# One copy of the row sums instead of two, with each 128-row scatter cut into two transfers of 64 rows

## What is computed

```python
def hier_moe(x, ...):                       # first block; the second one's is alike, with TOP_K 8 of 64
    ...                                     # e: expert of each (token, choice); c: its weight
    order = jnp.argsort(e_flat)             # pairs (token, choice) sorted by expert, padded
    def expert_block(args):
        xb, e = args
        hb = jax.nn.silu(xb @ w_gate[e]) * (xb @ w_up[e])
        return hb @ w_down[e]
    y = lax.map(expert_block, (x_pad, blk_expert)).reshape(P, D).astype(jnp.float32) * c_pad[:, None]
    out = jax.ops.segment_sum(y, tok_pad, num_segments=T + 1)[:T]
```

## Time and profile before

| | |
|---|---|
| time, median of 3 runs (us) | 3725.83 (3720.07 to 3726.52) |
| the profiled execution's own time (us) | 3724.51 |
| its span, first to last instruction (us) | 3722.8 |
| TensorE busy | 3232.0 us, 87% |
| VectorE, ScalarE, GpSimd busy | 42%, 19%, 20% |
| granted TensorE clock, mean | 0.934 |
| DMA, mean of the span | 152 GB/s |
| scatter L1767 | 103 transfers, 1756 ns of GpSimd each |
| gather L1746 | 109 transfers, 1069 ns of GpSimd each |

### The profile page before, as it was taken

How to read it: one execution, slowest core, us unless ns; L and a number is a source line. 1 busy time by engine, 2 the same in 40 slices (tenths; PEclk the granted TensorE clock), 3 DMA queues, 4 the chain that set the end, 5 groups by cost and what they waited for, 6 DMA issues and landing times. The chain is left out here.

```text
span 3722.8 us, 44810 instructions
## 1 busy us (share of the span) xinstructions
PE 3232.0 (87%) x14083; PEld 1609.1 (43%) x14084; DVE 1579.9 (42%) x2344; ACT 725.6 (19%) x1144; POOL 760.5 (20%) x952
## 2 busy tenths in 40 slices
PE   5999879995988996899869996798799999999991
PEld 2444345543655444433347774355333333333330
DVE  2222224434766123434436664234344444444445
ACT  2212213333544000111122320021011111111111
POOL 0000000002000000334510000000155555555554
PEclk9999989997999998799979997898899999999995
DMA  4111031113211123799650002202488999888875
GB/s 166 36 33 39 0 126 46 46 54 77 69 47 48 67 98 135 281 384 383 232 133 23 23 11 76 96 31 83 159 289 286 312 325 342 279 279 288 278 223 165
DMA packets 177131, 564.53 MB, mean 152 GB/s; under 512 B 18597, under 2 KB 88841, under 8 KB 139913
## 3 DMA queue, kind: packets, MB, share of 16 engines
q1 hardware_dynamic: 140888, 428.46, 30.4%
q0 software_dynamic: 35856, 133.74, 14.7%
q10 hardware_dynamic: 288, 1.05, 0.1%
HBM read 460.01 MB, written 103.20 MB: 151 GB/s over the span
## 5 line engine op out<-in xcount | busy, mean ns | idle before, releaser
L1814 PE MATMUL gu_ps<-w_gu,second 128*64 x1680 | 754.0, 602 | 12.9 <-DVE h L1877 7.7
L1817 PE MATMUL gu_ps<-h,second 128*64 128x512 f32 x1680 | 754.0, 602 | 0.0
L1814 PEld LDWEIGHTS gu_ps<-w_gu,second 128*64 128x64 f32 x1680 | 224.0, 138 | 454.5 <-issue 442.6
L1840 PE MATMUL y_ps<-w_dn,hid_t 128*64 x824 | 375.6, 598 | 0.3 <-issue 0.2
L1843 PE MATMUL y_ps<-second,hid_t 128*64 128x512 f32 x824 | 375.6, 598 | 0.0
L396 PE MATMUL ps<-second,wcol 128*128 128x512 f32 x768 | 333.7, 597 | 10.1 <-DMA wcol<-in_w_in_dram 7.7
L1877 DVE COPY h<-w_gu 128x4096 f32 x109 | 249.4, 2289 | 72.2 <-SPq L1694 71.9
L1742 POOL COPY idx<-moe_slot_tok 128x1 int32 (+1 forms) x109 | 25.1, 231 | 1024.9 <-POOLq L95 984.4
L396 PEld LDWEIGHTS ps<-second,wcol 128*128 128x128 f32 x768 | 147.0, 192 | 195.8 <-issue 187.9
L1817 PEld LDWEIGHTS gu_ps<-h,second 128*64 128x64 f32 x1680 | 224.0, 138 | 0.0
L1762 POOL TENSOR_TENSOR idx_y<-moe_slot_tok,moe_side 128x1 int32<-128x1 int32 x103 | 109.7, 1065 | 521.2 <-ACT second L1863 521.2
(11 more groups left out here) (430 smaller groups left out, 5085.4 us busy)
## 6 DMA issues: line engine op xcount, KB each, us to landing
w_gu<-in_w_gate_dram SPq DMA_DIRECT2D x96, 1024.0 KB, 8.1
w_gu<-in_w_up_dram SPq DMA_DIRECT2D x96, 1024.0 KB, 10.9
w_dn<-in_w_down_dram SPq DMA_DIRECT2D x96, 1024.0 KB, 10.5
wcol<-in_w_in_dram SPq DMA_DIRECT2D x12, 1024.0 KB, 5.3
qk_by_head<-stage SPq DMA_DIRECT2D x32, 384.0 KB, 3.3
qk<-qk_by_head SPq DMA_DIRECT2D x16, 768.0 KB, 7.6
token_sums<-zero POOLq DMA_DIRECT2D x19, 512.0 KB, 13.6
token_sums<-second SPq DMA_DIRECT2D x16, 512.0 KB, 2.6
```

The costliest lines, as they stand in the source:

```text
L1814: nc.tensor.matmul(gu_ps[0:PART, slot], x_t[:, slot, c, 0:PART], w_gu[:, bass.ds(ws, 1), :, c, :].rearrange("p o g n -> p (o g) n"), start ...
L1817: last = nc.tensor.matmul(gu_ps[PART:P, slot], x_t[:, slot, c, PART:P], st_gu[:, slot, :, c, :], start=c == 0, stop=c == C - 1)
L1840: nc.tensor.matmul(y_ps[0:PART, cs], hid_t[:, slot, c, 0:PART], w_dn[:, bass.ds(ws, 1), c, cs].rearrange("p o n -> p (o n)"), start=c == 0 ...
```

## The change

There is one copy of the sums, and no two transfers that add to it are in the air together. Each block's scatter is now two transfers of 64 rows (`part(slot, 0)` for partitions 0 to 63, `part(slot, 1)` for 64 to 127). The second is issued when the first has landed (`scatter_rest`), and the first of the next block when the second of this one has landed. `G.pair` holds the row numbers of both halves on partitions 0 to 63. The order within GpSimd's queue stays scatter, share, gather, and the second half comes behind the gather. The zeroing of the second copy and the adding of it are gone. ScalarE waits for 32 instead of 16 on `y_out` for each block. The last turn gathers one block more than before.

```diff
-def zero_second(pool, sum_d, zero, zero_out):
-
-    for t in range(T + 1):
-        pool.dma_start(sum_d[S + P + t * P:S + P + (t + 1) * P, :], zero).then_inc(zero_out, 16)
...
-def add_second(pool, sum_d, rows, row_in, both_in):
-    for t in range(T):
-        pool.wait_ge(row_in[t], 16)
-        pool.dma_start(rows[:, t, :], sum_d[S + P + t * P:S + P + (t + 1) * P, :],
-                       accum_op=ALU.add).then_inc(both_in[t], 16)
...
@@ take_sums
-                pe.wait_ge(both_in[t], 16)
+                pe.wait_ge(row_in[t], 16)
...
@@ dispatch
-            st(d.tensor_scalar(side[:], G.tok[:, 0:1], float(PART), float(S + P), ALU.is_ge, ALU.mult))
...
-            st(d.tensor_copy(G.side, side[:]))
...
+            for a in range(2):
+                st(d.tensor_copy(G.pair[:, 0:NB, a], empty[a * PART:(a + 1) * PART, :]))
...
@@ experts
-            def scatter(b, slot, landed, others):
+            def scatter(b, slot, own, others):
 
                 pool.wait_ge(y_taken, b + 2)
-                if landed is not None:
-                    pool.wait_ge(y_out[slot], landed)
-                g.tensor_tensor(idx_y[:, slot:slot + 1], G.slot_tok[:, bass.ds(b, 1)], G.side, ALU.add).then_inc(idx_y_ready, 1)
+                if own is not None:
+                    pool.wait_ge(y_out[slot], own)
+                g.tensor_copy(idx_y[:, slot, :], G.pair[:, bass.ds(b, 1), :].rearrange("p o a -> p (o a)")).then_inc(idx_y_ready, 1)
                 pool.wait_ge(idx_y_ready, 2 * b + 1)
                 if others is not None:
                     pool.wait_ge(y_out[1 - slot], others)
                 g.tensor_tensor(mark_y[:, slot:slot + 1], G.tok[:, 0:1], G.tok[:, 0:1], ALU.add).then_inc(idx_y_ready, 1)
-                g.indirect_dma_start(sum_d, bass.IndirectOffsetOnAxis(ap=idx_y[:, slot:slot + 1], axis=0),
-                                     y[:, slot, :], None, compute_op=ALU.add).then_inc(y_out[slot], 16)
+                part(slot, 0)
+
+            def scatter_rest(slot, landed):
+
+                pool.wait_ge(y_out[slot], landed)
+                g.tensor_tensor(mark_b[:, slot:slot + 1], G.tok[:, 0:1], G.tok[:, 0:1], ALU.add).then_inc(mark_ready, 1)
+                part(slot, 1)
+
+            def part(slot, a):
+                g.indirect_dma_start(sum_d, bass.IndirectOffsetOnAxis(ap=idx_y[:, slot, a:a + 1], axis=0),
+                                     y[a * PART:(a + 1) * PART, slot, :], None, compute_op=ALU.add).then_inc(y_out[slot], 16)
...
                     with pool.If(i <= n + 1):
-                        pool.wait_ge(x_turned, i)
-                        pool.wait_ge(share_in, i)
-                        gather(i + 1, 1 - slot)
-                        scatter(i - 2, slot, j * 16 + 16, j * 16 + (16 + 16 * u))
+                        scatter(i - 2, slot, j * 32 + 32, j * 32 + (32 + 32 * u))
                         keep_share(i, slot, j * 16 + 48)
...
+                        pool.wait_ge(x_turned, i + 1)
+                        pool.wait_ge(share_in, i + 1)
+                        gather(i + 2, slot)
+                        scatter_rest(slot, j * 32 + 48)
...
@@ final_norm
-            add_second(pool, sum_d, G.h, row_in, both_in)
...
-                v.wait_ge(both_in[t], 16)
+                v.wait_ge(row_in[t], 16)
```

More of the change, by code:

```diff
@@ L319, in _, with lru @@
                                 gain[:, :, None].to_broadcast([P, C, P]), ALU.mult).then_inc(taken, 1)
-def zero_second(pool, sum_d, zero, zero_out):
-    for t in range(T + 1):
-        pool.dma_start(sum_d[S + P + t * P:S + P + (t + 1) * P, :], zero).then_inc(zero_out, 16)
-def lru(nc, A, G, spare, sum_d):
+def lru(nc, A, G, spare):
     ph = phase(nc)
@@ L383, in _ @@
                 pool.dma_start(rows[S:S + P, :], zero[:, 0:rows.shape[1]]).then_inc(zero_out, 16)
-            zero_second(pool, sum_d, zero[:, 0:D], zero_out)
-            pool.wait_ge(zero_out, 16 * (len(spare) + T + 1))
+            pool.wait_ge(zero_out, 16 * len(spare))
         @block.tensor
@@ L1229, in take_sums @@
         row_in = ph.sems(" ".join(f"row_in{t}" for t in range(T)))
-        both_in = ph.sems(" ".join(f"both_in{t}" for t in range(T)))
         block = ph.ctx.enter_context(nc.Block())
@@ L1236, in _ @@
                 sp.dma_start(rows[:, t, :], sum_d[t * P:(t + 1) * P, :]).then_inc(row_in[t], 16)
-        @block.gpsimd
-        def _(pool):
-            add_second(pool, sum_d, rows, row_in, both_in)
         @block.tensor
@@ L1773, in _ @@
             n = pool.value_load(G.used, min_val=0, max_val=NB)
-            keep_share(0, 0, 16)
-            for i in range(1, 4):
-                pool.wait_ge(x_turned, i)
-                pool.wait_ge(share_in, i)
-                gather(i + 1, (i + 1) % 2)
+            for i in range(4):
                 if i >= 2:
-                    scatter(i - 2, i % 2, None, 16 if i == 3 else None)
+                    scatter(i - 2, i % 2, None, 32 if i == 3 else None)
                 keep_share(i, i % 2, i // 2 * 16 + 16)
+                pool.wait_ge(x_turned, i + 1)
+                pool.wait_ge(share_in, i + 1)
+                gather(i + 2, i % 2)
+                if i >= 2:
+                    scatter_rest(i % 2, 16)
             with pool.Fori(0, (NB - 1) // 2) as j:
@@ L1912, in moe_state @@
     G.w = w[:].rearrange("p (t k) -> p t k", k=K)
-    G.side = sb(f"moe_side{E}", [P, 1], I32)[:]
+    G.pair = sb(f"moe_pair{E}", [PART, P, 2], I32)[:]
     G.m = sb(f"moe_m{E}", [P, T, E])[:]
@@ L2228, in _, with pooling @@
             take_out(H - 1, H)
-def pooling(nc, A, G, sum_d):
+def pooling(nc, A, G):
     ph = phase(nc)
@@ L2247, in pooling @@
         p_ps = ph.ps("p_ps", [P, 2, S])
-        zero = ph.sb("zero", [P, D])
-        w_in, wp_in, u_ready, u_taken, m_ready, p_ready, p_taken, dve, cleared, zero_out = ph.sems(
-            "w_in wp_in u_ready u_taken m_ready p_ready p_taken dve cleared zero_out")
+        w_in, wp_in, u_ready, u_taken, m_ready, p_ready, p_taken, dve = ph.sems(
+            "w_in wp_in u_ready u_taken m_ready p_ready p_taken dve")
         block = ph.ctx.enter_context(nc.Block())
-        @block.gpsimd
-        def _(pool):
-            nc.gpsimd.memset(zero[:], 0.0).then_inc(cleared, 1)
-            pool.wait_ge(cleared, 1)
-            zero_second(pool, sum_d, zero[:], zero_out)
-            pool.wait_ge(zero_out, 16 * (T + 1))
         @block.sync
@@ L2628, in program @@
         rms_to_cols(nc, G, vec(G, "norm_mix_g"), G.u)
-        lru(nc, A, G, (rows1_d, rows2_d, sum_d), sum_d)
+        lru(nc, A, G, (rows1_d, rows2_d, sum_d))
         mla_project(nc, A, G, qk_d, v_d)
@@ L2653, in program @@
             hgrn(nc, A, G)
-            pooling(nc, A, G, sum_d)
+            pooling(nc, A, G)
             moe_state(nc, moe, G, K2, E2)
```

25 lines of the change are left out of this document (13 added, 12 removed).

## The result

| | before | after |
|---|---|---|
| median of the runs | 3726.2 us | 3968.7 us |
| range of the runs | 3720.1 to 3726.9 | 3948.7 to 3972.7 |
| ratio, 95% interval | | 1.0644 [1.0607, 1.0681] |
| span of the profiled execution | 3722.8 | 3966.3 |

The kernel became 6.4% slower. Forecast were 3714 us and a range of 3698 to 3800. The table by stretch of the kernel after, for the two expert stages (from the first gather to the reads that follow), shows where it went. The columns are: stretch, length, busy time (instructions) of TensorE, its weight loads, VectorE, ScalarE and GpSimd, then the share of TensorE's full clock that was granted, the DMA engines' busy share, GB/s.

What follows compares the result with a forecast made beforehand. TensorE was taken to set the pace of the second expert stage, DMA engines and weights partly that of the first. Terms: 3724.5 - 31 + 0.5 + 4 + 8 + 8 = 3714 us; range 3698 to 3800.

Steps and rivals of the forecast that it cites:

- take_sums: Start of `take_sums`: without the second copy's adds TensorE starts earlier, tiles run back to back; gain 12.7 us.
- final_norm: Last stage, without adding the second copy: GpSimd's last sum at 3705.8 against 3716.86; gain 11.1 us (8 to 12).
- pooling: Start of `pooling`, without the zeros beside its loads: TensorE starts at about 2297; gain 7 us (4 to 8.5).
- The chain: Expert stages, two landings a block: next issue after 9.6 us alone, 14.6 with weights streaming, against a 12.11 us period.
- recorded signs of being wrong: Scatters over 13 us per block, TensorE waiting on `xb` over 30 us, ScalarE waiting on a scatter, halves 6 us alone.
- The count: Second expert stage: five blocks meet streaming weights, 5 x 2.5 = 12.5 us, less 4: cost 8 us.
- The slip: Expert stages: a late issue delays the next gather, but some 4 us of this are free.
- rival C: Expert stages: chain replaces TensorE as bound where weights stream; 45 us in the first, 38 in the second; 3781; chance 0.28.
- D: Expert stages: 64 rows need as long as 128, so every block's chain exceeds 12.11 us; about 3970; chance 0.12.

Runs made afterwards that it cites:

- thinned weights: Changed kernel with the second expert stage's weight reloads cut to an eighth: 3753.4 us, ratio 1.0077; the kernel before with the same cut: 3725.9 us.

## Why the prediction was wrong, step by step

- **take_sums**: right in sign, too small (12.7 against 21.0). TensorE starts 3.4 us behind the reads (3.7 forecast). But I took 2.49 us a tile from the earlier trace rows as back to back, and its 0.52 is a wait for an add's landing, as the row says. After the change the first tiles wait for nothing, and VectorE's copies of them follow each other every 1.71 us:

```profile
1927.11 6.44 PE L1230 MATMUL tp<-ident,second 128*128 128x128 f32 x32 [25.59 <-DMA second<-token_sums]
...
1929.11 1.22 DVE L1237 COPY h<-tp 128x1024 f32<-128x1024 f32 x1 [22.63 <-PE tp L1230]
1930.82 1.23 DVE L1237 COPY h<-tp 128x1024 f32<-128x1024 f32 x1 [0.48 <-PE tp L1230]
1932.53 7.30 DVE L1237 COPY h<-tp 128x1024 f32<-128x1024 f32 x6 [0.48 <-PE tp L1230]
```

 Seven tiles at 1.71 are 12.0 us where 17.4 had been forecast; from the first tile's start to the last one's they took 10.4. The last 1.6 us go with the clock, by the two tables by stretch over the transposes, before and after:

```profile
1884.70:1906.80 22.10, 15.75 (x64) 12.55 (x64) 8.57 (x7) 0.00 (x0) 2.57 (x3) 0.50 0.92 204
```

```profile
1927.10:1938.60 11.50, 10.70 (x64) 9.49 (x64) 8.29 (x7) 0.00 (x0) 0.00 (x0) 0.75 0.73 296
```

 Before, TensorE worked with pauses and was granted 0.50 of its clock, the lower of its two levels, throughout; after, without pauses, 0.50 up to 1932 us and 1.00 from 1934 on. So the missed gain is first a wait read as work, and then a clock that rose earlier.
- **final_norm**: right, 11.3 against 11.1. VectorE starts on tile 0 4.7 us behind the first read and waits again for the bias, as worked out. **pooling**: 7 forecast, 8.2 at its start, of which 5.0 show in the stretch of this execution.
- **The chain**: this is the step that failed. Alone it was right: a half lands after 4.6 us (4.3 forecast). With weights streaming I had "the moving part is 10.2 - 2.4 = 7.8, its half 3.9, so 6.3"; in the block shown it is 5.1 of start, 2.9 of movement and 0.6 to the landing, 8.6. One subtraction, an idle start taken from a loaded landing, put a cost that is paid per transfer on the part that is paid per row. One stretch of the queues at the earlier trace rows would have told. The size of it, as an estimate: had every half started after 2.1 us, as with thinned weights, the mean chain would be 14.9 - 2 x (3.42 - 2.10) = 12.3 us, next to the 12.1 of before. Of the recorded signs of being wrong three came true: over 13 us a block, TensorE waiting on `xb`, ScalarE waiting on a scatter. The fourth, halves that take 6 us alone, did not.
- **The count**: "the five blocks at 10.2 us" was second to fail. I took the blocks in which the scatter meets the weights from the trace of before. There the scatter fell mostly into pauses of the weights (7 late starts of 79). The second half is issued some 7 us later and 48 of 79 start late. A new transfer falls elsewhere in the period. And a chain that becomes the bound shifts everything against the weights: the first halves, 32 of 79 late, are issued where the whole scatter had been. That this shift alone made them late is argued, not shown.
- **The slip**: "some 4 us of slip as free" was wrong too: a gather that is 4.4 us later costs 1.1 us a block, 85 us in the second stage.
- **A reading without consequence**: the 184 GB/s of the earlier trace rows aren't the scatter's own rate. GpSimd's queue moved 0.39 of the 0.46 MB there, 156 GB/s, and the weights' queue the rest.
- **What it costs**: rival C had the mechanism (landing, gather, landing replace TensorE as the bound where weights stream), its point of decision (12.11 us) and its sign; it priced 2.5 us in about 15 more blocks of the second stage than the forecast's five (and its sum, 3714 - 16 + 83, lost the five). In the mean of all 79 it was 2.8. Its first stage (45 us) is near the measured 47, in part by luck: it took 18 blocks that overrun a period of 12.1 with halves at 6.3, where that stage had a period of 13.4 before, 15.3 after and halves at 6.9 in the mean. With a half at 6.3 us C gives 3781; with 2.4 us more for each of two halves where weights stream, its heavy blocks take 14.6 + 4.8 = 19.4 us, 1.1 over the 18.3 above.
- **The range** ended at 3800. It had left out D with 0.12, the only rival that priced both halves of every block higher. D's 3970 against the measured 3968.7 is luck: 64 rows move faster than 128, and what was dear was the start.

## What to carry to other kernels

- Split a transfer's latency into start and movement at the load at which it will run, from the queue's packets in that very stretch. Only the movement shrinks with the size; a chain of two landings pays the start twice.
- Before a wait for a landing is put onto a queue, compare the whole loop of landings on it with the period, at the loaded price. Here it was 12.1 us against 14.9, and the 37 us saved elsewhere were no match for 103 rounds of it.
- Here the second copy was cheap, since it kept the transfers independent: what it costs at the ends (zeroing, the final add) was 37 us, of which the last version got 21 back by moving the zeroing to where GpSimd has time and reading the copy with plain loads.

## What was unexpected in the hardware

- A scatter issued by GpSimd begins to move either about 2.0 to 2.2 us after its issue or, while another queue keeps the DMA engines busy beyond that time (0.97 of their time in the stretch shown), after some 4.8 (3.5 to 5.8 singly). The late start doesn't depend on the rows (over all starts 3.42 us in the mean with 64, 3.36 with 128) and hardly on the other queue's packet size (means of those over 4.3 us: 4.96, and 4.92 with half of it). A long issue makes a start late too, 3.9 us with the DMA engines idle.
- Issuing 64 rows takes nearly as long as 128: 1.43 to 1.47 us against 1.61, and up to 3.3 beside VectorE's copy.
- TensorE's clock adds to a stall: in the second stage the same matmuls were busy for 1031 us at a granted 0.92, in place of 970 at 0.98, and 970 again at 0.98 when most of the waits were gone (thinned weights).
